# Two layers of latent attention: its low-rank query and key products with 128 output rows each, and the last layer without context queries

## What is computed

```python
A_HEADS, A_NOPE, A_ROPE, A_V = 4, 64, 32, 96      # Q_LORA = 256, KV_LORA = 128

def mla_queries(cq, g_qn, w_uq, rope):
    q = (rmsnorm(cq, g_qn) @ w_uq).reshape(B, N, A_HEADS, A_NOPE + A_ROPE).transpose(0, 2, 1, 3)
    qn, qr = q[..., :A_NOPE], q[..., A_NOPE:]
    if rope is not None:
        qr = apply_rope(qr, *rope)
    return qn, qr
...
for l in range(DEPTH):                            # DEPTH = 2
    last = l == DEPTH - 1
    ...
    qn, qr = mla_queries(cq, g_q_norm[l], w_uq[l], rope_lat)
    y_a = merge_heads(blocked_attend(qn, qr, (lat_keys, ctx_keys)))
    ...
    if not last:
        qn_c, qr_c = mla_queries(cqc, g_q_norm[l], w_uq[l], None)
        y_ac = merge_heads(softmax_attend(qn_c, qr_c, (ctx_keys,)))
```

## Time and profile before

| | us |
|---|---|
| median of 3 runs | 3623.95 (3618.31 to 3626.76) |
| profiled execution, its own time | 3622.27 |
| its span in the trace | 3620.5 |
| query, key and value products, first layer | 165.49 to 195.67 |
| the four weight blocks, second layer | 1211.77 to 1249.54 |
| query, key and value products, second layer | 1252.32 to 1282.49 |

### The profile page before, as it was taken

How to read it: one execution, slowest core, us unless ns; L and a number is a source line. 1 busy time by engine, 2 the same in 40 slices (tenths; PEclk the granted TensorE clock), 3 DMA queues, 4 the chain that set the end, 5 groups by cost and what they waited for, 6 DMA issues and landing times. The chain is left out here.

```text
span 3620.5 us, 52487 instructions
## 1 busy us (share of the span) xinstructions
PE 3278.1 (91%) x20898; PEld 2866.3 (79%) x20898; DVE 1779.8 (49%) x2649; ACT 1108.8 (31%) x1647; POOL 275.5 (8%) x234
## 2 busy tenths in 40 slices
PE   1999986999997899879999699889999899889997
PEld 1668775888886578758887697789999897789997
DVE  8547578554545647553333434544343434444343
ACT  2243223232232243223333333233222432233222
POOL 2000101001001000111111200010101100000101
PEclk9999888999998999889999899999999999999998
DMA  6101023322323101012222111122222211122322
GB/s 243 59 9 59 25 83 116 117 104 104 116 104 145 58 20 62 11 59 93 93 93 81 66 48 41 38 74 88 98 91 89 77 42 44 51 76 82 104 82 87
DMA packets 79090, 283.40 MB, mean 78 GB/s; under 512 B 10584, under 2 KB 10712, under 8 KB 77280
## 3 DMA queue, kind: packets, MB, share of 16 engines
q1 hardware_dynamic: 74912, 264.48, 20.7%
q0 software_dynamic: 3168, 11.31, 0.9%
q10 hardware_dynamic: 864, 5.57, 0.4%
HBM read 279.20 MB, written 2.10 MB: 78 GB/s over the span
## 5 line engine op out<-in xcount | busy, mean ns | idle before, releaser
L311 PE MATMUL ps<-h_hi,hi_ring 128*128 128x264 f32 (+2 forms) x4208 | 1344.9, 320 | 99.8 <-DVE h_lo L601 42.7
L311 PE MATMUL ps<-h_lo,hi_ring 128*128 128x264 f32 (+2 forms) x4208 | 1312.8, 312 | 0.0
L311 PE MATMUL ps<-h_hi,lo_ring 128*128 128x264 f32 (+2 forms) x4208 | 1310.5, 311 | 0.0
L240 DVE TENSOR_TENSOR lo_ring<-ring,hi_ring 128x1024 fp32r<-128x1024 f32 (+1 forms) x414 | 491.7, 1188 | 1036.2 <-ACT hi_ring L230 1035.3
L311 PEld LDWEIGHTS ps<-h_hi,hi_ring 128*128 128x128 f32 (+1 forms) x4208 | 796.6, 189 | 186.6 <-issue 108.7
L311 PEld LDWEIGHTS ps<-h_lo,hi_ring 128*128 128x128 f32 (+1 forms) x4208 | 798.2, 190 | 50.5 <-issue 3.4
L311 PEld LDWEIGHTS ps<-h_hi,lo_ring 128*128 128x128 f32 (+1 forms) x4208 | 794.5, 189 | 47.0
L230 ACT ACTIVATE hi_ring<-ring 128x1024 fp32r<-128x1024 f32 (+1 forms) x414 | 424.5, 1025 | 1265.1 <-PE ps L311 1244.2
L311 PE MATMUL ps<-hid_hi,hi_ring 128*128 128x512 f32 (+1 forms) x1472 | 473.4, 322 | 2.6 <-DVE hid_lo L839 1.7
L311 PE MATMUL ps<-hid_lo,hi_ring 128*128 128x512 f32 (+1 forms) x1472 | 474.2, 322 | 0.0
L311 PE MATMUL ps<-hid_hi,lo_ring 128*128 128x512 f32 (+1 forms) x1472 | 474.2, 322 | 0.0
(11 more groups left out here) (277 smaller groups left out, 2998.1 us busy)
## 6 DMA issues: line engine op xcount, KB each, us to landing
ring<-weights_dram SPq DMA_DIRECT2D x350, 512.0 KB, 3.2
mod_ring<-w_mod_dram SPq DMA_DIRECT2D x64, 512.0 KB, 4.1
ring<-weights_dram SPq DMA_DIRECT2D x64, 384.0 KB, 2.9
arena<-w_mod_dram SPq DMA_DIRECT2D x32, 512.0 KB, 3.4
x<-x_dram SPq DMA_DIRECT2D x1, 3072.0 KB, 16.2
arena<-c_rows_dram ACTq DMA_DIRECT2D x3, 1024.0 KB, 7.2
arena<-ret_decay_dram POOLq DMA_DIRECT2D x2, 1056.0 KB, 7.1
silu_rows<-c_rows_dram ACTq DMA_DIRECT2D x2, 1024.0 KB, 5.3
```

The lines of the kernel that those rows point to most:

```text
L240: self.nc.vector.tensor_tensor(self.lo_ring[:, g % SPLIT, 0:w], self.ring[:, g % RING, 0:w], self.hi_ring[:, g % SPLIT, 0:w], ALU.subtract ...
L311: ins = nc.tensor.matmul(out[0:m, c:c + n], w, a[:, t0:t0 + n], start=first and k == 0 and p == 0, stop=last and k == kts - 1 and p == 2)
```

## The change

It replaces the per-head products of `latent_attention` by products with 128 output rows.

- The query weights are laid out anew by the DMAs: `rope` holds the 32 rotary columns of all four heads (128 columns), `swap` the same with halves swapped, `nope` the 64 other columns of the four heads (two times 128). PE makes rope, nope 0 (heads 0 and 1), swap, nope 1 (heads 2 and 3), each into its own PSUM buffer, with no wait for a copy between them.
- ACT, and no longer DVE, copies the 64 rows of each head out with the scale (`heads_in`, line 1274), and in the first layer also the 32 rotary rows of the context queries, four copies of 32x256 (L1283).
- DVE turns four heads at once: one step of 128x512 against the cosine table (L1346), one against the sine table (L1349), and then four sums of 32x512, one per head, which wait only once (L1352).
- Keys are two products of 128 rows, each for two heads; ACT copies them as four times 64x768 as before.
- The tables are loaded four times, once for each group of 32 partitions, and the query weights are gathered: 14 DMAs on POOL's queue instead of 5.
- With `nq = ALL if ctx_queries else LAT`, the second layer makes the two `cq` blocks, their squares, norm and queries over 512 columns instead of 768.
- The counters `qk_psum` and `qk_copied` become nine counters, one for each thing waited for. The value products now wait for DVE's rotary sums (`q_rope_ready`), whose PSUM buffers they write.

```diff
+    nq = ALL if ctx_queries else LAT
+    group = lambda h: slice(h * A_ROPE, (h + 1) * A_ROPE)
+    pair_rows = lambda h: slice(h % 2 * A_NOPE, (h % 2 + 1) * A_NOPE)
...
-            pool.dma_start(cos[rot, :], dram["rope_cos"]).then_inc(tables.sem, 16)
-            pool.dma_start(sin[rot, :], dram["rope_sin"]).then_inc(tables.sem, 16)
-            pool.dma_start(sin[A_QK:P, :], dram["rope_sin"]).then_inc(tables.sem, 16)
-            pool.dma_start(w_uq, dram["w_uq"][l]).then_inc(lora_in.sem, 16)
+            for h in range(A_HEADS):
+                pool.dma_start(cos[group(h), :], dram["rope_cos"]).then_inc(tables.sem, 16)
+                pool.dma_start(sin[group(h), :], dram["rope_sin"]).then_inc(tables.sem, 16)
+            by_head = dram["w_uq"][l][:, 0:2 * A_HEADS * A_QK].rearrange("p (k h n) -> p k h n", k=2, h=A_HEADS)
+            for k in range(2):
+                pool.dma_start(nope[:, k, :].rearrange("p (h n) -> p h n", h=A_HEADS),
+                               by_head[:, k, :, 0:A_NOPE]).then_inc(lora_in.sem, 16)
+                pool.dma_start(rope[:, k, :].rearrange("p (h n) -> p h n", h=A_HEADS),
+                               by_head[:, k, :, A_NOPE:A_QK]).then_inc(lora_in.sem, 16)
+            pool.dma_start(swap.rearrange("p k n -> p (k n)"),
+                           dram["w_uq"][l][:, 2 * A_HEADS * A_QK:BLOCK]).then_inc(lora_in.sem, 16)
             pool.dma_start(w_ukv, dram["w_ukv"][l]).then_inc(lora_in.sem, 16)
...
-                product_parts(nc, core.buf(j), w, KT, acts, ALL).then_inc(core.done, 1)
+                product_parts(nc, core.buf(j), w, KT, acts, nq if j < 2 else ALL).then_inc(core.done, 1)
...
-            for h in range(A_HEADS):
-                if h == 1:
-                    pe.wait_ge(root.sem, root.at(2))
-                if h >= 2:
-                    pe.wait_ge(qk_copied.sem, qk_copied.at(h - 1))
-                product(nc, core.buf4(2 * h), [main[:, k, h * A_QK:(h + 1) * A_QK] for k in range(2)],
-                        [cq[:, k, :] for k in range(2)], ALL, A_QK)
-                last = product(nc, core.buf4(2 * h + 1), [swap[:, k, h * A_ROPE:(h + 1) * A_ROPE] for k in range(2)],
-                               [cq[:, k, :] for k in range(2)], LAT, A_ROPE, row=A_NOPE)
-                last.then_inc(qk_psum.sem, 1)
+            queries = [cq[:, k, :] for k in range(2)]
+            product(nc, core.buf4(2), [rope[:, k, :] for k in range(2)], queries, nq, P).then_inc(rope_psum.sem, 1)
+            product(nc, core.buf4(0), [nope[:, k, 0:P] for k in range(2)], queries, nq, P).then_inc(nope_psum.sem, 1)
+            pe.wait_ge(root.sem, root.at(2))
+            product(nc, core.buf4(3), [swap[:, k, :] for k in range(2)], queries, LAT, P).then_inc(rope_psum.sem, 1)
+            product(nc, core.buf4(1), [nope[:, k, P:2 * P] for k in range(2)], queries, nq, P).then_inc(nope_psum.sem, 1)
             pe.wait_ge(normed.sem, normed.at(2))
...
+            for n in range(2):
+                pe.wait_ge(nope_in.sem, nope_in.at(n + 1))
+                product(nc, core.buf4(n), [wkv[:, 2 * n * A_NOPE:(2 * n + 2) * A_NOPE]], [ckv[:, 0, :]], ALL,
+                        P).then_inc(k_psum.sem, 1)
+            pe.wait_ge(rope_in.sem, rope_in.at(1))
+            if ctx_queries:
+                pe.wait_ge(rope_ctx_in.sem, rope_ctx_in.at(1))
...
+            def heads_in(n, dst, tokens, factor, done):
+                for h in (2 * n, 2 * n + 1):
+                    last = nc.scalar.activation(dst[0:A_NOPE, h, 0:tokens], core.buf4(n)[pair_rows(h), 0:tokens],
+                                                ACT.Copy, scale=factor)
+                last.then_inc(done.sem, 1)
...
-            step(nc.vector.reciprocal(rstd[:, 0, :], rstd[:, 0, :]))
+            step(nc.vector.reciprocal(rstd[:, 0, 0:nq], rstd[:, 0, 0:nq]))
...
+            dve.wait_ge(rope_psum.sem, rope_psum.at(1))
+            step(nc.vector.scalar_tensor_tensor(work[:, 1, 0:LAT], core.buf4(2)[:, 0:LAT], scale, cos, ALU.mult,
+                                                ALU.mult))
+            dve.wait_ge(rope_psum.sem, rope_psum.at(2))
+            step(nc.vector.scalar_tensor_tensor(work[:, 0, 0:LAT], core.buf4(3)[:, 0:LAT], scale, sin, ALU.mult,
+                                                ALU.mult))
             for h in range(A_HEADS):
-                dve.wait_ge(qk_psum.sem, qk_psum.at(h + 1))
-                main, swap = core.buf4(2 * h), core.buf4(2 * h + 1)
-                step(nc.vector.tensor_scalar(qt[0:A_QK, h, :], main[0:A_QK, 0:ALL], scale, None, ALU.mult))
...
+                last = nc.vector.tensor_tensor(qt[rot, h, 0:LAT], work[group(h), 0, 0:LAT], work[group(h), 1, 0:LAT],
+                                               ALU.add)
+            last.then_inc(rope_in.sem, 1)
```

More of the change, by code:

```diff
@@ L1104, in latent_attention @@
     w_uq = probs_t.rearrange("p a b -> p (a b)")[:, 0:BLOCK]
+    nope = w_uq[:, 0:2 * A_HEADS * A_NOPE].rearrange("p (k n) -> p k n", k=2)
+    rope = w_uq[:, 2 * A_HEADS * A_NOPE:2 * A_HEADS * A_QK].rearrange("p (k n) -> p k n", k=2)
+    swap = w_uq[:, 2 * A_HEADS * A_QK:BLOCK].rearrange("p (k n) -> p k n", k=2)
     top, total, inv = a(1, 32)[:, 0, :], a(1, 32)[:, 0, :], a(1, 32)[:, 0, :]
@@ L1176, in _ @@
-            pe.wait_ge(normed.sem, normed.at(2))
-            for h in range(A_HEADS):
-                pe.wait_ge(qk_copied.sem, qk_copied.at(A_HEADS - 1 + h // 2))
-                product(nc, core.buf4(h), [wkv[:, h * A_NOPE:(h + 1) * A_NOPE]], [ckv[:, 0, :]], ALL,
-                        A_NOPE).then_inc(qk_psum.sem, 1)
+            pe.wait_ge(lora_in.sem, lora_in.at(96))
+            wkv = w_ukv
+            queries = [cq[:, k, :] for k in range(2)]
+            product(nc, core.buf4(2), [rope[:, k, :] for k in range(2)], queries, nq, P).then_inc(rope_psum.sem, 1)
@@ L1187, in _ @@
-            pe.wait_ge(qk_copied.sem, qk_copied.at(2 * A_HEADS + TT))
+                last.then_inc(v_psum.sem, 1)
+            pe.wait_ge(k_in.sem, k_in.at(2))
+            pe.wait_ge(v_in.sem, v_in.at(TT))
             pe.wait_ge(rotated.sem, rotated.at(1))
@@ L1245, in _ @@
                     act.wait_ge(summed.sem, summed.at(1))
[L1246 to L1248 removed]
+                n = nq if j < 2 else ALL
+                nc.scalar.activation(work[:, j % 2, 0:n], core.buf(j)[:, 0:n], ACT.Square).then_inc(squared.sem, 1)
+                nc.scalar.activation(first[:, j, 0:n], core.buf(j)[:, 0:n], ACT.Copy).then_inc(core.free.sem, 1)
+            nc.scalar.activation(rstd[:, 0, 0:nq], core.buf4(2)[:, 0:nq], ACT.Sqrt, bias=core.eps[:, 0:1],
                                  scale=1.0 / Q_LORA).then_inc(root.sem, 1)
@@ L1255, in _ @@
                                  scale=1.0 / KV_LORA).then_inc(root.sem, 1)
-            act.wait_ge(qk_copied.sem, qk_copied.at(A_HEADS))
-            for h in range(A_HEADS):
-                act.wait_ge(qk_psum.sem, qk_psum.at(A_HEADS + h + 1))
-                nc.scalar.activation(kt[0:A_NOPE, h, :], core.buf4(h)[0:A_NOPE, 0:ALL],
-                                     ACT.Copy).then_inc(qk_copied.sem, 1)
+            def heads_in(n, dst, tokens, factor, done):
[3 more added lines that the diff above has]
+                last.then_inc(done.sem, 1)
+            act.wait_ge(nope_psum.sem, nope_psum.at(1))
+            heads_in(0, qt, nq, scale, nope_in)
+            if ctx_queries:
+                act.wait_ge(rope_psum.sem, rope_psum.at(1))
+                for h in range(A_HEADS):
+                    last = nc.scalar.activation(qt[rot, h, LAT:ALL], core.buf4(2)[group(h), LAT:ALL], ACT.Copy,
+                                                scale=scale)
+                last.then_inc(rope_ctx_in.sem, 1)
+            act.wait_ge(nope_psum.sem, nope_psum.at(2))
+            heads_in(1, qt, nq, scale, nope_in)
+            for n in range(2):
+                act.wait_ge(k_psum.sem, k_psum.at(n + 1))
+                heads_in(n, kt, ALL, 1.0, k_in)
             for t in range(TT):
-                act.wait_ge(qk_psum.sem, qk_psum.at(2 * A_HEADS + t + 1))
+                act.wait_ge(v_psum.sem, v_psum.at(t + 1))
                 nc.scalar.activation(v[:, t, :], core.ps[:, 4 + t % 4, 0:A_HEADS * A_V],
-                                     ACT.Copy).then_inc(qk_copied.sem, 1)
+                                     ACT.Copy).then_inc(v_in.sem, 1)
             def exponents(u):
@@ L1357, in latent_attention @@
     n = len(units)
-    for s, k in ((tables, 48), (lora_in, 32), (rotated, 1), (squared, 3), (summed, 2), (root, 2), (normed, 2), (qk_psum, 2 * A_HEADS + TT),
-                 (qk_copied, 2 * A_HEADS + TT), (scored, n), (peak, n), (expd, n), (turned, n), (turned_in, n),
+    for s, k in ((tables, 32 * A_HEADS), (lora_in, 96), (rotated, 1), (squared, 3), (summed, 2), (root, 2), (normed, 2),
+                 (rope_psum, 2), (nope_psum, 2), (k_psum, 2), (v_psum, TT), (rope_in, 1),
```

(1 more changed line is left out.)

32 lines of the change are left out of this document (11 added, 21 removed).

## The result

The changed kernel took 3588.88 us (median of 4 runs, 3587.58 to 3593.01), the kernel before 3622.01 (4 runs, 3618.31 to 3626.76) on the same chip. The profiled execution of the changed kernel took 3589.21 us, with a span of 3587.4.

A forecast was written before the change was run, and what follows sets the result against it. PE, busy 91% of the span, was taken as the bound; 12.4 + 5.6 + 1.45 + 14.3 = 33.7 us less than 3622.27 gave 3588.6, or 3590.2 from the median: forecast 3590 us, range 3581 to 3602.

The forecast's parts named there:

- What bounds the kernel: Whole kernel: PE, busy 91% of the span; each microsecond the attention pipeline starts earlier comes off the span unless given back.
- First layer, 12.4 us: First layer, first query product to scores: scores start at 17.8 us instead of 30.18, 12.4 us less.
- the lower end of the forecast: Product pairs at 2.57 us and copies overlapping by their tails: the two stretches gain 1.3 us more, 3587.
- Two weight blocks, 5.6 us: Second layer, ahead of the queries: two weight blocks lose their 256-column pieces, 5.6 us less; lower clock left out.
- The sign of being right that asked for 5.6 us in each of the two blocks: Second layer: blocks 0 and 1 would take 5.6 us each if the forecast was right.
- Ones to the first query product, 1.45 us: Second layer, product against ones to queries: 12.3 us instead of 13.8, the wait passing from DVE to ACT's copy; 1.45 less.
- Second layer, 14.3 us: Second layer, first query product to scores: 15.9 us instead of 30.17, with PE waiting 1.2 us for DVE; 14.3 less.
- The sum: Whole kernel: 12.4 + 5.6 + 1.45 + 14.3 = 33.7 us less, forecast 3590 us.
- Output rows cost after all: Rival, PE's products: packed ones no faster than narrow ones, about 12 us gain remaining, 3612 us; chance 0.02.
- Gathers land late: Rival, query weight DMAs: PE's first query product waits; half late 3597 to 3624, chance 0.03; slower, chance 0.03.
- Gain given back by the clock: Rival, after this function: later clock returns and dearer turning steps take back 6 to 12 us, 3596 to 3602; chance 0.13.
- the case p = 0.4: Late gathers, each piece of at most 256 bytes costing 0.4 us on a DMA engine: time would be 3642 us.

The follow-up runs named there:

- e6_keys_on_pool: Changed kernel with the turning of the rotary key and its four copies on POOL instead of DVE; 3587.85 us (one run).
- e7_both: Changed kernel with keys turned on POOL and the second layer's value products in PSUM banks 5, 7, 4, 6; 3589.72 us (median of 4), 0.9914 of before.
- e5_values_early: Changed kernel with the second layer's value products in PSUM banks 5, 7, 4, 6, the first two not waiting for DVE's sums; 3587.59 us (one run).
- after_again: Changed kernel once more, unaltered, for a second profile; 3591.76 us (median of 4), 0.9894 of before on its chip.
- e4_fine_pieces: Changed kernel with two more gathers of 8192 pieces of 32 bytes per layer, which the query products wait for; 3591.22 us (one run).
- before_again: Kernel before the change once more, unaltered, for a second profile; 3622.54 us (one run).

## Why the prediction was right

*What bounds the kernel.* Right. Each microsecond off the stretches came off the span, and the parts behind them gave back nothing that the repeats don't show too.

*First layer, 12.4 us.* It gained 12.7. Its scores came at 17.47 instead of 17.8. The 0.3 us lie in PE's products: swap and nope 1 took 4.29 us (from ACT's start at 170.89 to that at 175.18) instead of 1.83 + 2.74 = 4.57. That is the pace of the 2.57 us for a pair in the lower end of the forecast, though the long row that the prediction points at doesn't give it (6656 columns in 11.96 us would make it 2.76). The other terms checked one by one: records of 128 output rows at the old pace, turning steps at 0.69 (0.68 assumed), ACT's 32x256 copies at 0.38 (0.35 guessed), the wait for the second pair of copies there and short.

*Two weight blocks, 5.6 us.* This is the term that was mis-sized in the first pair of profiles, where 4.6 us was gained, and its step is the one that left the clock out because it "can only add to this". It took from it. Timeline of PE in the changed kernel, first block of the second layer:

```profile
1203.02 0.77 PE L311 MATMUL ps<-h_hi,hi_ring 128*128 128x512 f32 x1 [5.21 <-PEq L1011]
...
1208.28 0.63 PE L311 MATMUL ps<-h_hi,hi_ring 128*128 128x512 f32 x1
1208.70 0.58 PE L311 MATMUL ps<-h_lo,hi_ring 128*128 128x512 f32 x1
1209.12 0.40 PE L311 MATMUL ps<-h_hi,lo_ring 128*128 128x512 f32 x1
```

And the windows over the block in the kernel before, with the granted clock in the third figure from the end:

```profile
1211.77:1215.20 3.43, 3.43 (x10) 2.86 (x11) 0.00 (x0) 0.00 (x0) 2.59 (x5) 0.52 0.77 277
1215.20:1216.20 1.00, 1.00 (x8) 0.87 (x7) 0.00 (x0) 0.00 (x0) 0.00 (x0) 1.00 1.11 291
```

After the same idle time of 5.21 us, matmuls are 0.43 us apart until 1209.1 in the changed kernel, that is for 6.1 us, and in the kernel before for about 3.3 (the clock's mean is still 0.52 up to 1215.20 and 1.00 from there). So block 0 took 8.38 us (1203.02 to 1211.40) against 5.44 for block 1. My argument needed a lower clock that lasts until the same piece of work; it lasts a time, and not always the same one. The sign of being right that asked for 5.6 us in each of the two blocks therefore failed for block 0. `e6_keys_on_pool` had the lower clock for about 3.4 us and its blocks took 20.96, `e7_both` for 3.3 and its blocks took 20.92: against the kernel before, with the same 3.3 us, that is 5.9 us less, a little more than the 5.6. So the price of the pieces was 0.3 us short, and the 2.8 us more at half clock in the first pair hid 1.3 us of the gain. Over all profiles, blocks with 768 columns took 26.78 to 27.28 us (three, mean 26.96) and those with 512 took 20.92 to 22.20 (eight, mean 21.55): 5.4 us less on the mean, near the 5.6.

*Ones to the first query product, 1.45 us.* Measured 1.46, with the wait passed to ACT's copy as told.

*Second layer, 14.3 us.* It gained 14.1. Both the wait for DVE's sums (1.32, forecast 1.2) and the narrow lead of the turned keys (0.33, forecast 0.4) were there. `e5_values_early` and `e7_both` confirm that these two are next in line.

*The sum.* The four touched terms come to 32.9 us in the first pair of profiles and, with the mean of the blocks, to 33.7. The median moved by 33.1. That the whole came within 0.6 us is partly luck: the long parts behind the stretches differ by 5 to 6 us between two executions of one kernel, and here their -4.0 and +4.2 us cancelled. On the chip of `after_again` the medians of the same two kernels are 35.8 us apart.

*The rivals.* "Output rows cost after all": excluded by 601 ns. "Gathers land late": excluded by margins of 28 and 23 us, and `e4_fine_pieces` shows that its price was at least eight times too high for a piece, a wrong step of a case with a small chance, which cost the forecast nothing. "Gain given back by the clock": the mechanism is real, and moves the long parts by some 6 us in either direction from one execution to the next, but I put it forward as something that the change brings, and it stands in two executions of the same kernel. I didn't foresee that it would also take from the blocks.

*Slips in the working that changed nothing.* By its own formula the case p = 0.4 gives 3641 us, not 3642; the gain starts to melt at p = 0.18 from 3590 us, not from 3597; and the chances inside 3581 to 3602 add up to 0.875 (0.70 + 0.13 + half of 0.09), not 0.86.

## What to carry to other kernels

Where PE is the bound, count columns, not rows: products that share their moving operand are worth packing to 128 output rows, and with them the elementwise steps behind them, which cost the same over 128 partitions as over 32. Look at the engine that copies and turns what PE makes as well, since its path can take the place of PE's: the second stretch was 27.88 us with fewer columns but unpacked, 22.86 with packed products and DVE doing the copies too, 16.07 with all. No run here packed the products and left the turning steps head by head, so what those steps are worth by themselves is not shown. And before an edit that takes a wait away, ask who is next behind it: here two waits for DVE stood behind one another, and removing the first gave 0.18 us.

## What the runs showed of the hardware beyond what was expected

A wait of PE can cost more than its length: after one of 3.68 us the granted clock was 0.50 for the next 5.6 us or so, and the two key products right behind it, which take 1.4 us each at the full clock, took 5.25 us together. After waits of 1.32 and 2.40 us it stayed at 1.00.

The length of the wait doesn't settle it. At one place that all kernels share, the first layer's MLP, where PE waits for `hid_lo` (L839), nine of the eleven profiles have a wait of over 2 us. In four of them the clock was 0.50 over the next 2 us, after waits of 2.42 (`before_again`), 2.57, 2.51 and 2.49 us; in four it was 1.00, after 2.36, 2.38, 2.59 and 2.74 us (`e5_values_early`); in the ninth 0.61, after 2.08.

How long the lower clock lasts after the same idle time of 5.21 or 5.22 us, ahead of the second layer's weight blocks, isn't fixed either: from about 3.3 us to 6.1 over the eleven profiles. Both, over all the places where PE idles, may be what makes parts with the same instructions differ by 6 us; beyond these two places this was seen in the clock's mean only.

DMA pieces of 32 bytes cost at most 0.02 us each on a DMA engine, and they hold up the issuing engine: POOL stood idle 8.37 us before it issued a second gather of 8192 pieces.
